# Two transformer blocks on one core: whole-width norms by column sums, part of their squares and additions on other engines, spreads, rotations and the meta-token transpose moved

## The reference, cut to what matters

```
# first block
h = rms_norm(x, g_attn_pre) * (1 + scale_a) + shift_a        # scale, shift, gate: silu(c) @ w_ada + b_ada
... = split(h @ w_in)                                         # differential and indexed sparse attention
x = x + gate_a * rms_norm(mixed @ w_o, g_attn_post)           # norm "attn_post"
h = rms_norm(x, g_ffn_pre) * (1 + scale_f) + shift_f          # norm "ffn_pre"
x = x + gate_f * rms_norm((silu(h @ w_gate) * (h @ w_up)) @ w_down, g_ffn_post)   # norm "ffn_post"
# second block, on h = concat([meta_tokens, x])
proj = rmsnorm(h, mix_norm_g) @ w_in                          # norm "mix"
q_a, k_a = rmsnorm per head of 128                            # norms "na_q0", "na_q1", "na_k0", "na_k1"
q = rmsnorm(cq) @ w_q_up; kv = rmsnorm(ckv) @ w_kv_up         # norm "latent"
q, k = rmsnorm per head of 192, 64 of them rotated (rope)     # norms "mla_q", "mla_k"
h = h + concat([rmsnorm(out_a), rmsnorm(out_b)]) @ w_out      # norms "na_out", "mla_out"
h = h + (silu(conv(rmsnorm(h) @ w_gate)) * (rmsnorm(h) @ w_up)) @ w_down          # norm "ffn2"
```

## Time and profile before

| | |
|---|---|
| median of three runs | 2745.94 us |
| the profiled execution, its own time | 2744.68 us |
| its span in the profile | 2742.9 us |
| TensorE (PE) busy | 2557.4 us, 93% |
| VectorE (DVE), ScalarE (ACT), GpSimd (POOL) busy | 53%, 37%, 11% |
| granted TensorE clock, mean | 0.963 |
| bytes moved, mean rate | 504 MB, 184 GB/s |

### The profile page before, as it was taken

One profiled execution on the slowest core, in us unless ns is written; L12 is line 12 of the kernel. 1 busy time (PEld: TensorE's weight loads), 2 busy tenths in 40 slices (PEclk: granted clock), 3 DMA queues, 4 the chain that ended last, 5 costly groups with the idle time before them and its releaser, 6 DMA issues.

```text
span 2742.9 us, 47702 instructions
## 1 busy us (share of the span) xinstructions
PE 2557.4 (93%) x19896; PEld 2388.0 (87%) x19896; DVE 1440.1 (53%) x1913; ACT 1025.9 (37%) x1299; POOL 309.8 (11%) x409
## 2 busy tenths in 40 slices
PE   5999988969999999999959998998799999999998
PEld 3898847949999999999948896776799999999998
DVE  3577666866664444344454454644555555553443
ACT  3533244334433343333333335413344444443332
POOL 4000121420000000011123002103200000000000
PEclk8999999989999999999979999989999999999999
DMA  8777866936785555555444341311355555555553
GB/s 302 273 266 262 297 228 243 329 119 231 246 289 185 184 183 184 169 178 186 141 131 139 116 139 62 108 62 62 124 183 184 184 182 182 175 182 168 183 184 107
DMA packets 263862, 504.00 MB, mean 184 GB/s; under 512 B 17168, under 2 KB 26299, under 8 KB 263483
## 3 DMA queue, kind: packets, MB, share of 16 engines
q1 hardware_dynamic: 256288, 494.57, 54.5%
q10 hardware_dynamic: 7467, 7.92, 0.9%
HBM read 498.05 MB, written 2.10 MB: 182 GB/s over the span
## 4 chain that ended last, share of the span: by engine, by line
PE 76%; DVE 10%; ACT 5%; issue 4%; DMA 3%; POOL 1%; ACTq 1%; DVEq 0%; SPq 0%; POOLq 0%
PE bank L1931 22%; PE bank L1933 22%; PE bank L1932 22%; ACT w_hi L820 3%; DVE w_lo L1286 3%; DMA raw<-in_w_in 1%; PE bank L2029 1%; PE bank L1966 1%; DMA staged<-in_w_ada 1%; PE bank L2054 1%; DVE tmp L1423 1%; DVE ada_acc L1314 1%; PE bank L2210 1%; PE bank L2255 0%; ACT x_hi L948 0%
## 5 line engine op out<-in xcount | busy, mean ns | idle before, releaser
L1286 DVE TENSOR_TENSOR w_lo<-raw,w_hi 128x2048 fp32r<-128x2048 f32 (+3 forms) x386 | 861.1, 2231 | 1011.4 <-ACT w_hi L820 1011.0
L1931 PE MATMUL bank<-x_hi,w_hi 128*128 128x256 f32 (+2 forms) x4608 | 1323.2, 287 | 57.0 <-DVE w_lo L1286 17.8
L1932 PE MATMUL bank<-x_lo,w_hi 128*128 128x256 f32 (+2 forms) x4608 | 1315.1, 285 | 0.0
L1933 PE MATMUL bank<-x_hi,w_lo 128*128 128x256 f32 (+2 forms) x4608 | 1314.0, 285 | 0.0
L820 ACT ACTIVATE w_hi<-raw 128x2048 fp32r<-128x2048 f32 (+3 forms) x386 | 718.5, 1862 | 1112.0 <-PE bank L1933 970.8
L1931 PEld LDWEIGHTS bank<-x_hi,w_hi 128*128 128x128 f32 x4608 | 881.5, 191 | 91.5 <-DVE w_lo L1286 37.8
L1933 PEld LDWEIGHTS bank<-x_hi,w_lo 128*128 128x128 f32 x4608 | 882.8, 192 | 0.0
L1932 PEld LDWEIGHTS bank<-x_lo,w_hi 128*128 128x128 f32 x4608 | 879.0, 191 | 1.0 <-issue 1.0
L1931 PE MATMUL bank<-hid_hi,w_hi 128*128 128x256 f32 x1408 | 401.0, 285 | 7.9 <-POOL hid_lo L689 6.6
L1933 PE MATMUL bank<-hid_hi,w_lo 128*128 128x256 f32 x1408 | 400.2, 284 | 0.0
L1932 PE MATMUL bank<-hid_lo,w_hi 128*128 128x256 f32 x1408 | 400.1, 284 | 0.0
(11 more groups left out here) (301 smaller groups left out, 1512.7 us busy)
## 6 DMA issues: line engine op xcount, KB each, us to landing
raw<-in_w_ada SPq DMA_DIRECT2D x88, 1024.0 KB, 5.8
raw<-in_w_gate SPq DMA_DIRECT2D x88, 1024.0 KB, 5.2
raw<-in_w_up SPq DMA_DIRECT2D x88, 1024.0 KB, 5.2
raw<-in_w_in SPq DMA_DIRECT2D x68, 1024.0 KB, 7.2
raw<-in_w_down SPq DMA_DIRECT2D x64, 1024.0 KB, 5.1
raw<-in_w_down SPq DMA_DIRECT2D x32, 768.0 KB, 4.4
raw<-in_w_o SPq DMA_DIRECT2D x16, 1024.0 KB, 6.6
raw<-in_w_out SPq DMA_DIRECT2D x16, 1024.0 KB, 5.2
```

Of the source, the lines that this page charges most:

```text
L1286: dve.tensor_tensor(w_lo[ps][:, 0:width], raw[slot][:, 0:width], w_hi[ps][:, 0:width], ALU.subtract).then_inc(raw_free[slot], 1)
L1931: pe.matmul(out, wh[:, k, c], hi(k0 + k), start=a0, stop=False)
L1932: pe.matmul(out, wh[:, k, c], lo(k0 + k), start=False, stop=False)
L1933: ins = pe.matmul(out, wl_[:, k, c], hi(k0 + k), start=False, stop=z)
```

## The change

It does the following, in the order of the program.

- Norms attn_post, ffn_post, ffn2 (the last 4 tiles) and na_out, mla_out (the last tile): the squares of these tiles are made by ScalarE, for attn_post and ffn_post straight from PSUM before the copy, into a ring of four buffers (sq4, which overlies sq and tmp), and TensorE sums them as columns of their own; GpSimd's presum ends 4 (1) tiles earlier.
- Norms ffn_pre and mix: squares go into the ring of four, TensorE sums each tile as columns (one product per 128 positions and tile, into banks 7, 6 and 4, each with its own accumulation) and starts as soon as the first square is there; statistics run on columns.
- Five of the 16 additions to x_res (tiles 1, 4, 7, 10, 13) go to VectorE, between the applications.
- `dense` behind ffn_pre, mix, mla_out and ffn2 waits for x_lo tile by tile within its first output tile, no longer four at a time.
- The meta tokens are transposed and copied behind block 0 of the first down projection.
- Both down projections wait for the hidden activation unit by unit in their block 0.
- Spreads of the four head norms come one unit later (before unit 3), their application behind unit 4. The rotations come one unit later too: 1 and 2 before unit 0 of out2 block 0, 3 and 4 before unit 1, 5 to 8 in block 1; the query statistics are transposed before TensorE waits for the last rotation, and the statistics of mla_k begin one block earlier.
- `heads(16, 24)` and `heads(24, 32)` begin with the scores of two heads; transposes of values, high parts of the latents and meta-token scores follow them.

```diff
+        sq4 = place("sq4", [P, 4, N2], at=sq_at)
+        DVE_ADDS = (1, 4, 7, 10, 13)
-             branch_a_ssq)
+             branch_a_ssq, direct=4)
...
-               mod[:, SH_F + t:SH_F + t + 1]) for t in range(KT)], True)
+               mod[:, SH_F + t:SH_F + t + 1]) for t in range(KT)], True, column=True)
...
+        def column_bank(b):
+            return bank[(7, 6, 4)[b]]
...
-            return bank[5 if len(norms[name]["groups"]) == 1 else 4 + g % 4][0:rows, 0:n]
+            return bank[5 if len(norms[name]["groups"]) == 1 else 7 - g % 4][0:rows, 0:n]
...
# gpsimd
-                with pool.Fori(0, 4) as i:
+                with pool.Fori(0, 3) as i:
...
             def add_branch(name, branch, first):
                 for t in range(KT):
+                    if t in DVE_ADDS:
+                        continue
...
-                for h in range(8):
+                for h in range(7):
...
# scalar
+                if g1 > 16:
+                    name, out = ("na_out", na_out) if g1 == 24 else ("mla_out", mla_out)
+                    act.wait_ge(h_taken, g1)
+                    act.wait_ge(m_taken, g1 // 4 - 4)
+                    square_into(name, 0, out[:, 7, :])
...
+            def take_branch(branch, i, m, ssq):
+                if ssq:
+                    act.wait_ge(tile_done, t.value(m + 1))
+                    square_into(ssq, m, bank[m][:, 0:S])
+                take(m, lambda b: act.activation(branch[:, bass.ds(i * 4 + m, 1), :].rearrange(
+                    "p a n -> p (a n)"), b[:, 0:S], ACT.Copy))
...
+            loop(2, (4, 4, 1, 8, 4), lambda i: out1(i + 1))
+            out1(3, ssq="attn_post")
...
-            loop(4, (12, 4, 0, 12, 12), down1)
+            down1(0)
             for g in range(KT // 8):
                 act.wait_ge(x_turned, 8 + g + 1)
                 act.activation(x_res[:, 8 * g:8 * g + 8, S:N2], bank[5 + g % 2][:, 0:8 * META].rearrange(
                     "p (t n) -> p t n", t=8), ACT.Copy).then_inc(x_copied, 1)
+            loop(2, (12, 4, 0, 12, 12), lambda i: down1(i + 1))
+            down1(3, ssq="ffn_post")
...
+            act.wait_ge(n_lo, norm_end("mla_out", "split"))
+            for m in range(4):
+                act.wait_ge(bank_freed, 4 + 4 * (FREED_NA + 3) + m + 1)
+                square_into("ffn2", m, x_res[:, 12 + m, 0:NC])
...
# vector
+                        chain(*[dve.tensor_scalar(v[0:bn, b:b + 1], column_bank(b)[0:bn, 0:1], 1.0 / n["dim"], EPS,
+                                                  ALU.mult, ALU.add) for b, (_, bn) in enumerate(blocks(cols))])
...
+                    if add and k - 1 in DVE_ADDS:
+                        dve.wait_ge(n_app, first["use"] + k)
+                        dve.tensor_tensor(x_res[:, k - 1, 0:S], x_res[:, k - 1, 0:S], n["uses"][k - 1][1],
+                                          ALU.add).then_inc(added_dve, 1)
...
-                        elif q == 3:
+                        elif q == 4:
                             apply(name)
...
-            values2(13, 4)
-            heads(16, 24)
+            heads(16, 24, lambda: values2(13, 4))
...
-            rope_add(R2 + 1)
-            rope_sin(R2 + 3)
-            rope_add(R2 + 2)
-            rope_sin(R2 + 4)
...
+                if i < 2 and q:
+                    r = R2 + 4 * i + 2 * q
+                    rope_add(r - 1)
+                    if r + 1 <= R2 + 8:
+                        rope_sin(r + 1)
+                    rope_add(r)
+                    if r + 2 <= R2 + 8:
+                        rope_sin(r + 2)
...
# tensor
+                            if tile_ready and m == 0:
+                                pe.wait_ge(n_lo, norms[tile_ready]["first"]["split"] + 4 * j + k + 1)
...
+                    def columns(x, start, stop):
+                        for b, (b0, bn) in enumerate(width):
+                            ins = pe.matmul(column_bank(b)[0:bn, 0:1], x[:, b0:b0 + bn], one(), start=start, stop=stop)
+                        return ins
+                    direct = n["direct"] if n["presum"] is not None else len(n["groups"][0])
+                    if n["presum"] is not None:
+                        pe.wait_ge(n_presum, first["presum"] + 1 + len(n["groups"][0]) - direct)
+                        columns(n["presum"][:, 0, :], True, False)
...
+                    for k in range(direct):
+                        pe.wait_ge(n_sq, first["sq"] + k + 1)
+                        ins = columns(sq4[:, k % 4, :], n["presum"] is None and k == 0, k == direct - 1)
...
-            pe.wait_ge(hid_low, 4 + FT)
...
+            def hidden_ready(before):
+                def ready(j):
+                    k0, nk = K44[j]
+                    pe.wait_ge(hid_low, 4 + before + k0 + nk)
+                return ready
+            down(0, ready=hidden_ready(0))
             pe.wait_ge(meta_in, 32)
-            pe.wait_ge(n_app, norm_end("ffn_post", "use"))
             for g in range(KT // 8):
...
+            loop(3, (12, 4, 12), down)
             pe.wait_ge(x_copied, 10)
+            sums("ffn_post")
             sums("mix")
...
-                    elif q == 2:
+                    elif q == 3:
                         spread(name)
...
-                    rotate2(R2 + 1)
-                    rotate2(R2 + 2)
...
+                if i < 2:
+                    rotate2(R2 + 1 + 4 * i + 2 * q)
+                    rotate2(R2 + 2 + 4 * i + 2 * q)
...
                     collect("mla_k")
-                    pe.wait_ge(r_out, R2 + 9)
...
-            meta_scores(1, N2, bank[7])
-            heads(24, 32)
+            heads(24, 32, lambda: meta_scores(1, N2, bank[7]))
```

More of the change, by code:

```diff
@@ L384, in program, with added_before @@
         dve_chain, pool_chain = sem("dve_chain"), sem("pool_chain")
+        DVE_ADDS = (1, 4, 7, 10, 13)
+        def added_before(t):
+            return sum(k not in DVE_ADDS for k in range(t))
         SH_A, SC_A, GT_A, SH_F, SC_F, GT_F = (KT * j for j in range(6))
@@ L469, in square_ring @@
         def square_ring(name):
-            return sq_wide if norms[name]["n"] == N2 and name != "mix" else sq
+            return sq if name == "diff" else sq_wide if norms[name]["n"] == N2 and name != "mix" else sq4
+        def column_bank(b):
+            return bank[(7, 6, 4)[b]]
         def sum_bank(name):
@@ L1185, in _, with latents_high @@
                     act.dma_start(tmp[0:64, 1, :], a["positions_2"][0:1, :].broadcast_to([64, N2])).then_inc(pos2_in, 16)
-            for k in range(6):
-                act.wait_ge(n_app, norms["latent"]["first"]["use"] + k + 1)
-                act.activation(x_hi[:, 8 + k, :], latents[k], ACT.Copy).then_inc(lat_high, 1)
-            heads(16, 24)
+            def latents_high():
+                for k in range(6):
+                    act.wait_ge(n_app, norms["latent"]["first"]["use"] + k + 1)
+                    act.activation(x_hi[:, 8 + k, :], latents[k], ACT.Copy).then_inc(lat_high, 1)
+            heads(16, 24, latents_high)
             def take_queries(j):
@@ L1358, in statistics @@
                     v, h, y = newton[:, 0, 0:2], newton[:, 1, 0:2], rstd[:, 0:2]
-                elif n["presum"] is not None:
+                elif n["column"]:
                     k = len(blocks(cols))
@@ L1819, in out2_beside @@
                     statistics("mla_k", 0)
+                elif i < 2 or q == 0 or (i == 2 and q == 2):
+                    return
                 elif i == 2:
@@ L2008, in collect @@
                 first, cols, width, groups = n["first"], n["n"], blocks(n["n"]), len(n["groups"])
-                if n["presum"] is not None:
-                    pe.wait_ge(n_presum, first["presum"] + 1 + len(n["groups"][0]))
-                    for b, (b0, bn) in enumerate(width):
-                        ins = pe.matmul(bank[7][0:bn, b:b + 1], n["presum"][:, 0, b0:b0 + bn], one(), start=True,
-                                        stop=True)
-                    ins.then_inc(n_col, 1)
+                if n["column"]:
+                    def columns(x, start, stop):
[6 more added lines that the diff above has]
+                        columns(n["presum"][:, 0, :], True, False)
+                    else:
+                        pe.wait_ge(n_rstd, first["norm"])
+                    for k in range(direct):
+                        pe.wait_ge(n_sq, first["sq"] + k + 1)
+                        ins = columns(sq4[:, k % 4, :], n["presum"] is None and k == 0, k == direct - 1)
+                        if n["presum"] is None or k == direct - 1:
+                            ins.then_inc(n_col, 1)
                 else:
@@ L2048, in spread @@
                         pe.wait_ge(n_app, first["use"] + len([u for u in used if u <= g - 4]))
-                    if n["presum"] is not None or n["given"] is not None:
+                    if n["column"]:
                         for b, (b0, bn) in enumerate(width):
@@ L2344, in in2_beside @@
             def in2_beside(i, q):
-                if i == 0:
```

(7 more changed lines are left out.)

151 lines of the change are left out of this document (71 added, 80 removed).

## The result

The changed kernel takes 2694.54 us (median of four runs, 2692.96 to 2700.77) against 2745.33 us in the same comparison; the ratio is 0.982 (95% interval 0.980 to 0.984). The forecast was 2690, its range 2676 to 2706. The span of the profile fell from 2742.9 to 2693.6 us, by 49.3 where the sum had 55.5.

What follows compares the result with a forecast made beforehand. Only TensorE's idle time and its time at 1.2 GHz could shorten the kernel (busy 93%). Gains of 10.3, 10.4, 7.5, 9.3, 17.0 and 1.0 sum to 55.5 us off 2744.68: 2689.2, or 2690; range 2676 to 2706.

Steps and rivals of the forecast that it cites:

- Parts 1 and 2: Norms attn_post with ffn_pre, ffn_post with mix: shorter sums, Newton on columns and earlier dense start gain 10.3 and 10.4 us.
- the pass: In the column sums of ffn_pre and mix: a one-column product at 1.2 GHz costs 0.197 us.
- The form L2255: Full stationary tile against one column, back to back: nearest row for column sums staying at 1.2 GHz, 0.197 us each.
- The moved transposes: Meta-token transposes behind down block 0: 16 passes, 1.86 us at the low clock, about half at the high; cost 1.2.
- Rival B: Column sums of ffn_pre and mix bring the clock back to 2.4 GHz, saving 4 and 6 us: 2680; chance 0.15.
- Parts 3 and 4: Norms mla_out and ffn2 gain 7.5 us; down projections gain 9.3 from hidden-tile waits gone and clock regained.
- Part 5: Head-norm spreads and rotations later: waits 4.4 and 6.2, clock 3.6 and 3.4, less 0.6 for na_out: 17.0 us.
- The clock terms: Half the clock loss regained: 3.6 us at the spreads (bounds 0 and 7.1), 3.4 in out2 (0 and 6.7).
- Rival C: Clock gives nothing back at down projections, spreads and rotations (10.4 us), spreads' waits return (4.4): 2705; chance 0.25.
- Rival D: Low clock outlasts the norms at six places; slower from 111 us additional low clock, 2765 at 25 each; chance 0.03.
- Part 6: Neighbourhood and latent heads: new order gains the start and part of a hole, together 1.0 us, bounds 0 and 2.5.

Runs made afterwards that it cites:

- the run by quarters: Changed kernel, first dense block behind ffn_pre, mix, mla_out and ffn2 again waiting for four feature tiles at a time: 2707.43 us.
- the run with the down blocks alone: Kernel before the change, with only the first down block of both MLPs waiting unit by unit for its own hidden tiles: 2737.38 us.
- wide products: Changed kernel with an unused 256-column product ahead of each of the 24 one-column meta output products in the latent heads: 2701.05 us.
- dealing out the meta products: Changed kernel with the latent heads' 24 one-column meta output products placed behind the scores of the fourth, sixth and eighth head: 2700.67 us.
- the row sums: Changed kernel with ffn_pre and mix summed by rows instead of columns, begun as early, behind the first addition: 2686.12 us.
- the mixture: Changed kernel with two unused 256-column products ahead of each tile's column sums in ffn_pre and mix: 2708.27 us.

## Why the prediction was right, and where it was not

**Parts 1 and 2.** The steps came as written: attn_post's sums begin at once and end 2.4 us later, the first application to the end of ffn_pre's sums took 15.7 (14.2 forecast, 17.5 before), Newton gained 2.7 (2.5), and the start by tiles about 2.3 at each norm, by the run by quarters (2.0). The term that was mis-sized is the pass: 0.215 us in ffn_pre where 0.197 stood, and 1.08 us for the six passes of a tile in mix where 0.99 stood. The form L2255 was rightly chosen, but its 0.197 was not a price at 1.2 GHz. The clock fell 3.0 us after L2255 began; the 6.40 us at 0.50 in the earlier trace rows hold 28 passes, 0.23 us each, and where nearly all 48 ran at the low clock they took 11.33 us, 0.236 each (the second profile of the changed kernel). The moved transposes cost 0.7 where 1.2 stood; half of their 1.86 us, by the prediction's own words, would have been 0.9.

**Rival B** is out: the clock stood at 0.50 under all column sums of ffn_pre and mix. The nearer row decided rightly between the two. The rule of the Trainium skill (page "TensorE: Matmul & The Clock Gate", section "The HAM clock gate") that the prediction weighed, by which sustained activity releases the throttle, would have had it back; the trace disagrees, with 13.79 and 17.35 us of unbroken work at 0.50.

**Parts 3 and 4** were within a microsecond each, as the run with the down blocks alone bears out for part 4. There is no wait of TensorE for w_lo over 0.5 us in the two down blocks.

**Part 5.** The waits were right to the tenth (4.4 and 6.2, both shown by putting them back). The clock terms, taken as half of what the windows had lost, have the right sign and are no better known than the profiles repeat. Spreads, 3.6 forecast: 5.1 from before to after, 3.4 if the changed kernel's second profile is taken (6.8 us low, as in eight others), 8.5 or 6.8 by the run that puts them back. Rotations, 3.4 forecast: 3.4 from before to after, 5.1 by the run that puts them back.

**Rival C** did not come: the waits of the spreads are gone, and the clock gave back the 3.4 us of part 4 in full and 8.5 in part 5 where 7.0 stood. **Rival D** is out too: over the whole span the low time is 202 us where it was 206.

**Part 6 is the step that failed,** though the total stayed within its range. It said the new order gains 1.0, bounds 0 and 2.5, and counted holes alone. As a count of holes that is about right: at equal low time the new order gained 0 to 0.9 us in the neighbourhood heads and lost 0.4 in the latent ones. But the stages lost 6.9, outside the bounds: low time went from 6.8 to 13.7 us in the neighbourhood heads (1.8 us longer) and from 13.7 to 23.9 in the latent heads (5.1 us longer). The prediction's own have a low stretch of the latent heads, and no bound was set on it. Restoring either order, wide products and dealing out the meta products all left it between 24 and 34 us.

**What stays open.** The two kernels with the old code in these stages had 13.7 and 17.1 us of low clock in the latent heads, the twelve profiles of the changed kernel and its variants 17.1 to 34.1, most of them 23.9 or 27.3. Two profiles are few against a spread of 3.4 between two profiles of one program and of 17 between near relatives. Whether something in the change makes the return later or these two were early is not settled. Nor is why the row sums had the clock back and the mixture did not.

**A better version.** The row sums begun early beat both kernels: 2686.12 and, with the meta products dealt out, 2687.95. Row sums with Newton on columns were not tried; by the difference of 2.7 us between the two Newtons, less what it costs to turn the row into columns, they should keep up to 2.7 us more at each norm (an estimate).

## What to carry to other kernels

A sum over partitions by one-column products saves VectorE the row-wise links behind it, but here TensorE paid for it at half clock. Where such a sum stands in a chain, price wide passes over rows as well: they were faster by 1.4 us with two blocks of positions to a tile and by 5.8 with three. Cost the granted clock of every stage that a change shifts in time, also of those whose work it leaves alone. Where TensorE is busy through a stage, take half of the low time off before comparing two profiles: that tells a change of work from a change of clock; where it waits for others the sum does not hold. Moving a dependent step one unit later gave the waits that the trace showed for it in full, and some clock on top that varied between profiles.

## What the runs showed of the hardware that was not expected

- With TensorE 100% busy the granted clock stayed at 0.50 for 10.1 to 34.1 us at a time in the latent heads, among products of 272 columns, transposes and a few of one column; the same program had 23.9 us of it in one profile and 27.3 in another.
- Under row sums of 256 columns the clock was back 5.4 us after they began (5.2 in the kernel before); under column sums of the same squares it was not in 13.79 us, nor in 17.35 us at mix, nor in 20.36 us with 32 products of 256 columns among 64 passes of one column.
- A one-column pass over a full stationary tile took 0.12 us at PEclk 1.00 (16 in 1.93 us) and 0.215 to 0.246 us at 0.50.
- In the twelve profiles of the changed kernel and its variants, whose code is the same up to there, out1 ended between 556.9 and 565.2 us, with 44 to 61 us of low clock: a single profile's span is not the measure of a change of 8 us.
